# Three more means by split products: the first attention's output, the query latent, the second attention's output

## The reference, cut to what matters

```python
def rmsnorm(x, g):
    xf = x.astype(jnp.float32)
    y = xf * lax.rsqrt(jnp.mean(xf * xf, axis=-1, keepdims=True) + EPS)
    return (y * g.astype(jnp.float32)).astype(x.dtype)
...
y = jnp.concatenate([rmsnorm(ya, g[:A_WIDTH]), rmsnorm(yb, g[A_WIDTH:])], axis=-1) @ e_w_out[i]
...
q = (rmsnorm(cq, q_a_gain) @ w_uq)       # cq: the query latent, 384 wide
kv = (rmsnorm(ckv, kv_a_gain) @ w_ukv)
k_rope = rmsnorm(kr, k_gain[NOPE_DIM:])
...
y = jnp.concatenate([rmsnorm(yc, g[:C_WIDTH]), rmsnorm(yd, g[C_WIDTH:])], axis=-1) @ o_w_out[i]
```

## Time and profile before

| | us |
|---|---|
| median of 3 runs | 1103.95 (1103.93 to 1104.01) |
| the profiled execution | 1103.62 |
| its span, first to last instruction | 1101.8 |
| PE busy | 1091.3 (99%), 5148 matmul instructions |
| DVE busy | 557.4 (51%) |
| ACT busy | 426.1 (39%) |
| granted clock of PE | 1.000 |

### The profile page before, as it was taken

One profiled execution on the slowest core, in us unless ns is written; L12 is line 12 of the kernel. 1 busy time (PEld: TensorE's weight loads), 2 busy tenths in 40 slices (PEclk: granted clock), 3 DMA queues, 4 the chain that ended last, 5 costly groups with the idle time before them and its releaser, 6 DMA issues.

```text
span 1101.8 us, 13776 instructions
## 1 busy us (share of the span) xinstructions
PE 1091.3 (99%) x5148; PEld 882.0 (80%) x5148; DVE 557.4 (51%) x790; ACT 426.1 (39%) x679; POOL 104.0 (9%) x126
## 2 busy tenths in 40 slices
PE   9999999999999999999999999999999999999998
PEld 7787788888888888888878765788888888888887
DVE  6787967444344333242476589656334433453321
ACT  5756445333223222131456558545223322322110
POOL 6000000010001000000102023000001100100000
DMA  7513233333332323232233200233333233327431
GB/s 230 168 58 91 64 115 96 96 95 95 95 95 95 98 98 99 101 100 83 72 93 101 83 17 2 77 119 92 102 98 101 80 114 95 95 77 175 112 126 46
DMA packets 103241, 106.00 MB, mean 96 GB/s; under 512 B 26267, under 2 KB 79968, under 8 KB 103200
## 3 DMA queue, kind: packets, MB, share of 16 engines
q1 hardware_dynamic: 85488, 103.04, 30.2%
q10 hardware_dynamic: 16656, 2.10, 1.1%
q0 software_dynamic: 1056, 0.30, 0.1%
HBM read 101.23 MB, written 2.10 MB: 94 GB/s over the span
## 4 chain that ended last, share of the span: by engine, by line
PE 47%; DVE 2%; ACT 1%; issue 0%; ACTq 0%
PE ps L1766 15%; PE ps L1767 14%; PE ps L1768 14%; PE ps L2260 1%; PE ps L2232 1%; ACT o_p L1118 0%; PE ps L2246 0%; DVE tiny L1667 0%; DVE o_k L1595 0%; PE ps L2173 0%; PE ps L1818 0%; PE ps L1799 0%; PE ps L1811 0%; DVE o_p L1695 0%; PE ps L2103 0%
## 5 line engine op out<-in xcount | busy, mean ns | idle before, releaser
L1186 DVE TENSOR_TENSOR w_lo<-raw,w_hi 128x1024 fp32r<-128x1024 f32 (+2 forms) x192 | 224.6, 1175 | 397.6 <-ACT w_hi L727 396.0
L727 ACT ACTIVATE w_hi<-raw 128x1024 fp32r<-128x1024 f32 (+2 forms) x192 | 194.3, 1016 | 446.7 <-PE ps L1768 417.0
L1766 PE MATMUL ps<-h_hi,w_hi 128*128 128x512 f32 x912 | 357.6, 392 | 0.0
L1767 PE MATMUL ps<-h_lo,w_hi 128*128 128x512 f32 x912 | 355.1, 389 | 0.0
L1768 PE MATMUL ps<-h_hi,w_lo 128*128 128x512 f32 x912 | 355.1, 389 | 0.0
L1766 PEld LDWEIGHTS ps<-h_hi,w_hi 128*128 128x128 f32 x912 | 171.2, 188 | 39.5 <-issue 4.4
L1768 PEld LDWEIGHTS ps<-h_hi,w_lo 128*128 128x128 f32 x912 | 171.2, 188 | 36.0
L1767 PEld LDWEIGHTS ps<-h_lo,w_hi 128*128 128x128 f32 x912 | 171.2, 188 | 35.5 <-issue 0.5
L610 POOL TENSOR_TENSOR ffn_t<-ffn_t,row_scale 128x512 f32<-128x512 f32 x40 | 50.9, 1294 | 604.7 <-ACT ffn_t L941 604.7
L1767 PE MATMUL ps<-w_lo,act_hi 128*128 128x512 f32 (+1 forms) x178 | 68.8, 387 | 0.0
L1768 PE MATMUL ps<-w_hi,act_lo 128*128 128x512 f32 (+1 forms) x178 | 68.8, 387 | 0.0
(11 more groups left out here) (334 smaller groups left out, 1169.8 us busy)
## 6 DMA issues: line engine op xcount, KB each, us to landing
raw<-in_w_ffn_in SPq DMA_DIRECT2D x88, 512.0 KB, 3.5
raw<-in_w_ffn_out SPq DMA_DIRECT2D x44, 512.0 KB, 3.7
raw<-in_e_w_in SPq DMA_DIRECT2D x17, 512.0 KB, 3.8
raw<-in_o_w_in SPq DMA_DIRECT2D x8, 512.0 KB, 3.6
raw<-in_o_w_out SPq DMA_DIRECT2D x8, 512.0 KB, 3.5
raw<-in_e_w_out SPq DMA_DIRECT2D x8, 256.0 KB, 3.8
raw<-in_e_w_out SPq DMA_DIRECT2D x4, 512.0 KB, 4.1
out_tok<-x_blocks ACTq DMA_DIRECT2D x16, 128.0 KB, 2.5
```

The lines of the kernel that those rows point to most:

```text
L727: ins = act.activation(dst, src, ACT.Copy)
L1186: ins = TT(dst, src, high, ALU.subtract)
L1766: MM(dst, st_hi, mv_hi, start=start, stop=False)
L1767: MM(dst, st_hi, mv_lo, start=False, stop=False)
```

## The change

The sums of M_EB, M_CQ and M_OD get tiles for their high and low parts (`eb_sq`, `cq_sq`, `od_sq`). On ACT and DVE each gets a `sum_hi` and a `sum_lo`, ahead of the conversion of weights that stood there. On PE the three plain means become split means. That of M_EB moves from before `ab(3)` to the middle of `ab(3)`; that of M_CQ moves from after load 97 to after load 98; that of M_OD stays.

```diff
+    eb_sq = at("eb_sq", [P, 2, S], F32R, R + 20 * K)
+    cq_sq = at("cq_sq", [P, 2, S], F32R, R + 13 * K)
+    od_sq = at("od_sq", [P, 2, S], F32R, R + 16 * K)
...
-    SPLIT_SUMS = (M_MIX0, M_EQ, M_EQ + 1, M_EQ + 2, M_EQ + 3, M_EK, M_EA, M_FFN0, M_MIX1, M_CKV, M_KR, M_FFN1)
+    SPLIT_SUMS = (M_MIX0, M_EQ, M_EQ + 1, M_EQ + 2, M_EQ + 3, M_EK, M_EB, M_EA, M_FFN0, M_MIX1, M_CQ, M_CKV, M_KR, M_OD, M_FFN1)
...
@@ ACT
         through(15)
         e_out(3)
+        act.wait_ge(yb_summed, 4)
+        sum_hi(M_EB, acc[:, :])
         through(16)
         rms(M_EB, ps[:, 5, :], 512)
...
             act.activation(sq[:, j % 2, :], cq[:, j, :], ACT.Square).then_inc(cq_squared, 1)
+        act.wait_ge(cq_summed, 3)
+        sum_hi(M_CQ, acc[:, :])
         through(O_CQ + 4)
         rms(M_CQ, ps[:, 3, :], 384)
...
         through(113)
         o_out(3)
+        act.wait_ge(yd_summed, 4)
+        sum_hi(M_OD, acc[:, :])
         through(O_OUT)
         rms(M_OD, ps[:, 7, :], 512)
...
@@ DVE
         e_sum(2)
         e_sum(3)
+        dve.wait_ge(yb_summed, 4)
+        sum_lo(M_EB, acc[:, :])
         through(15)
         through(16)
         r = rms(M_EB, ps[:, 5, :], 512)
...
         sum_squares(cq_squared, cq_summed, 3, M_MIX1)
+        dve.wait_ge(cq_summed, 3)
+        sum_lo(M_CQ, acc[:, :])
         through(O_CQ + 4)
         r = rms(M_CQ, ps[:, 3, :], 384)
...
         yd_sum(3)
+        dve.wait_ge(yd_summed, 4)
+        sum_lo(M_OD, acc[:, :])
         through(O_OUT)
         r = rms(M_OD, ps[:, 7, :], 512)
...
@@ PE
         ab(2, lambda: e_values(3))
-        pe.wait_ge(yb_summed, 4)
-        mean(M_EB, 5, ones, acc[:, :])
-        ab(3)
+        ab(3, lambda: split_mean(M_EB, 5, ones_r))
...
         def cq_mean():
-            pe.wait_ge(cq_summed, 3)
-            mean(M_CQ, 3, ones, acc[:, :])
+            split_mean(M_CQ, 3, ones_r)
...
                  extra=kr_parts if j == 3 else None)
-            if j == 1:
+            if j == 2:
                 cq_mean()
...
             if (j, part) == (1, 1):
-                pe.wait_ge(yd_summed, 4)
-                mean(M_OD, 7, ones, acc[:, :])
+                split_mean(M_OD, 7, ones_r)
```

More of the change, by code:

```diff
@@ L404, in sum_parts @@
             return act_hi[:, FT - 1, :], act_lo[:, FT - 1, :]
-        t = {M_MIX0: mix0_sq, M_EK: ek_sq, M_EA: ea_sq, M_MIX1: mix1_sq, M_CKV: ckv_sq, M_KR: kr_sq}[m]
+        t = {M_MIX0: mix0_sq, M_EK: ek_sq, M_EA: ea_sq, M_MIX1: mix1_sq, M_CKV: ckv_sq, M_KR: kr_sq,
+             M_EB: eb_sq, M_CQ: cq_sq, M_OD: od_sq}[m]
         return t[:, 0, :], t[:, 1, :]
```

## The result

The changed kernel takes 1107.66 us in the median of 7 runs (1105.97 to 1109.73), the kernel before 1103.93 (1103.38 to 1104.01). The ratio is 1.0031, 95% interval 1.0022 to 1.0040. So it is slower, by 3.7 us; the forecast was 2.9. The median hides something that the single runs show, with the granted clock of PE beside them: three runs at 1.000 took 1105.97, 1106.11 and 1106.62, three at 0.998 took 1107.66, 1107.83 and 1108.09, one at 0.997 took 1109.73. The change costs about 2.2 us by itself, and in 4 of 7 runs a slower stretch of PE's clock comes on top.

A forecast was written before the change was run, and what follows sets the result against it. PE, busy 99% of the span, was taken as the bound, with other engines' chains close behind. +2.2 (M_EB) + 1.1 (M_CQ) - 0.4 (M_OD) = +2.9 us on 1103.95 gave 1106.8; range 1105.0 to 1107.9.

The forecast's parts named there:

- the clock: Rival: PE's 2.5 us stand before the first output load drops its clock, +2 us, 1108.8; chance 0.03.
- a further wait: Rival: later conversions or transfer order add 0.5 to 1.5 us on top, about 1107.9; chance 0.08.
- Prices: At the three means: split holds PE 0.46 us, plain 0.86; root starts 0.66 after a split mean, 1.16 after a plain.
- M_EB, a loss of 2.2: Mean moved into ab(3): root 2.24 us later, chain to yb_lo without slack, PE waits before the first output load.
- M_CQ, a loss of 1.1: Mean moved after load 98: PE leads by 1.56 us, chain 1.18 later; two meetings turn the lead into a loss.
- first meeting: Join product L2119 waits about 1.0 us for kr; PE's lead shrinks from 1.56 to 0.5.
- At the second: Second four of eight transposes wait for M_KR's step, 1.18 us later through load 104; lead 0.5 becomes lag 1.1.
- Part 2: The forecast's M_CQ section: loss of 1.1 us, with ends of -0.5 and +1.3.
- M_OD, a gain of 0.4: Mean split but not moved: root 0.40 us earlier, gain between 0.35 and 0.45.
- Added work at nothing: Six short ACT and DVE instructions end weight conversions 0.7 to 1.4 us later, costing nothing; at most 1.4 if wrong.
- rival with slack everywhere: Chains at yb_lo and the transposes have slack, PE keeps all savings: gain 2.4 us, 1101.6; chance 0.05.
- half case: Only M_EB's chain bites, load 104's chain absorbs 1.2: +1.3, 1105.2, chance 0.16; mirror, only M_CQ's: +0.3, 0.03.

The follow-up runs named there:

- e1: Kernel before with only M_EB's edit (split mean, moved to the middle of ab(3)): 1107.37 us, ratio 1.0032.
- e3: Kernel before with only M_OD's mean split, at its old place: 1103.53 us, ratio 0.9997.
- e6: Kernel before with only M_EB's mean split, left before ab(3): 1104.43 us, ratio 1.0006.
- e7: Kernel before with only M_CQ's mean split, left after load 97: 1105.04 us, ratio 1.0012.
- e9: Kernel before with only the conversion of load 104 moved behind the first steps of the norms: 1103.94 us, ratio 1.0001.
- e5: Kernel before with M_CQ's edit (split, after load 98) and load 104's conversion moved behind the norms' first steps: 1103.21 us, ratio 0.9995.
- e2: Kernel before with only M_CQ's edit (split mean, moved to after load 98): 1104.50 us, ratio 1.0005.
- e4: Changed kernel plus ten unused matmuls between ab(3) and the first output load: 1106.23 us, ratio 1.0024.
- e11: Changed kernel plus five unused matmuls ahead of the first output load: 1106.04 us, ratio 1.0019.
- e8: Kernel before with M_OD split, M_CQ plain in the middle of load 98, and load 104's conversion moved: 1102.29 us, ratio 0.9986.
- e10: Kernel before with M_OD split and M_CQ plain in the middle of load 98, load 104's conversion not moved: 1103.37 us, ratio 0.9996.

## Why the prediction was right, point by point

The direction, the places and the order of size came out. That the measured 1107.66 also lies within the range of 1105.0 to 1107.9, near its upper end, is in part luck: two errors went opposite ways. At full clock the change costs 2.2 us where 2.9 were forecast (near 1106.1, just under the forecast's own 1106.3 to 1107.3), and then the clock, a rival at 0.03, lifted the median by 1.6. The upper part of the range had been left for a further wait, and none came.

- *Prices.* Forecast were 0.46 us of PE for a split mean and a root 0.66 after its start. The changed kernel has 0.49, 0.47 and 0.48, and the root follows after 0.68, 0.67 and 0.68. Shown.
- *M_EB, a loss of 2.2.* The chain's shift is 2.24, the stall 2.46 and PE's own delay 2.40 - 0.14 = 2.26 in the profiled run. e1 has +1.8 in its only run at full clock; 2.24 less the 0.28 of the second attention would be 2.0, which is within the spread of single runs. The slack of at most 0.15 in that chain was the reading that decided, and it held.
- *M_CQ, a loss of 1.1.* Mis-sized: 0.66 in the trace. The distance to the kernel before is 4.01 us at the sum and 4.67 at the first `cq_hi` matmul. The first meeting is right (a lead of 0.49, 0.5 forecast, and a stall of 0.95). At the second, the chain is 0.74 late, not 1.18. The link that gave the rest back is POOL's: from its first copy to ACT's conversion passed 577.31 - 576.05 = 1.26 us before and 582.08 - 581.25 = 0.83 after. The first two rows are of the kernel before, the third is of the changed one:

```profile
575.40 1.23 DVE L1186 TENSOR_TENSOR w_lo<-raw,w_hi 128x1024 fp32r<-128x1024 f32 x1 [0.26 <-ACT w_hi L727]
...
576.05 0.66 POOL L634 COPY raw<-raw 128x48 f32<-128x48 f32 x1 [25.46 <-DMA raw<-in_o_w_uq]
```

```profile
579.13 1.23 DVE L1196 TENSOR_TENSOR w_lo<-raw,w_hi 128x1024 fp32r<-128x1024 f32 x1 [0.19 <-ACT w_hi L731]
```

  Before, POOL's copy starts while DVE subtracts to get `w_lo` of load 103, and ends at 576.71, 0.08 after DVE; in the changed kernel DVE has been done for 0.9 us, and the same copy takes 0.22. The traces of all the kernels agree. In the six that leave M_CQ at its place (before, e1, e3, e6, e7, e9) the copy meets this subtraction, takes from 0.37 to 0.80, and ends 0.08 after it each time; in the seven that move it, it does not and takes 0.22 or 0.23. So the claim of Part 2 that each link had waited only for the one before was wrong here: POOL had waited for DVE. The prediction carried a shift unchanged through six links on four engines, and named the chain over SP and POOL as what could absorb it, but not how. e5 and e9 together show that the second loss comes over load 104: with it moved the stall is gone, and the move alone gives nothing.
- *M_OD, a gain of 0.4.* 0.38 in the trace (the distance to the kernel before goes from 4.40 at the mean to 4.02 at the weight load), 0.3 in e3.
- *Added work at nothing.* No wait of PE in the trace names a converted weight.
- *The second attention, not in the sum: a gain of 0.28.* The kernel before has one more wait of PE for ACT's `o_p`. ACT stands for 0.21 us ahead of that instruction, for nothing that the profile shows:

```profile
675.18 0.69 ACT L1118 ACTIVATE o_p<-ps,tiny 128x512 f32<-128x512 f32 x1 [0.21 <-issue]
...
676.10 2.22 PE L2232 MATMUL ps<-o_k,o_q 128*64 128x448 f32 x16 [0.28 <-ACT o_p L1118]
```

  In the changed kernel both are gone, and the distance to the kernel before falls there from 4.68 to 4.40. The same holds for e1, e2, e4 to e7 and e11; e3, e8, e9 and e10 have both as before. What tells the two groups apart is whether ACT and DVE have each been given an instruction more ahead of this place, not how late PE comes. Why that helps is open.
- *The clock.* Here the forecast was wrong. It was a rival at 0.03, and it came in 4 of 7 runs, at 1.5 to 2.0 us (three runs) and about 3.5 us (one). Its price of +2 was nearly right: ten matmuls were assumed and eight were slow in the profiled run. The chance was taken from a stall of 1 us that had left the clock alone, which says nothing on one of 2.5. Without it the median would have been near 1106.1, 0.7 under the forecast of 1106.8: 0.44 by M_CQ and 0.28 by the second attention.
- *The rival with slack everywhere* and the *half case* fall by the waits for `yb_lo` and `rs`.

## What to carry to other kernels

Where the matrix engine is busy for 99%, a cheaper instruction is worth its saving only if nothing on the other engines starts from its end; so price a move by following its result to the next tile that the matrix engine reads, and compare the two arrival times before counting the saving. The one edit of the three that left its instruction in place, with its input long ready, was the one that paid. And a stall has two prices, its length and what the clock does afterwards: five useless matmuls in a stall of 2.5 us took 1.6 us off the median. Last, a delay does not pass through a chain unchanged where one of its links was being held by an engine outside the chain.

## What the runs showed of the hardware

Over all runs, the three kernels with a stall of 2.4 to 2.5 us in mid-stream (the changed one, e1, e7) had a clock below 1.000 in 14 of 24 runs. The kernel before and the nine others, whose stalls in mid-stream are at most 1.4 us (the wait at 54 us, in all of them), had it in 6 of the 185 runs whose clock is recorded. Three runs at the lower clock were profiled. In two, the changed kernel's and e1's, the slow stretch follows the stall of 2.5 us; in the third, e2's, it follows the wait at 54 us, so a shorter stall can do it too, only seldom. The loss in such a run is 1.1 to 2.5 us, and in two runs at clock 0.997 about 3.5; why it is twice as long in these is open, as none of them was profiled, and what decides whether a given run falls is not shown either. So a kernel with such a stall also has a wider spread: 3.8 us in the changed one, 0.6 in the 7 runs of the kernel before beside it.

A short copy on POOL (128x48, 0.22 us by itself) that started during DVE's subtraction of two tiles (`w_lo<-raw,w_hi`, 1.23 us) ended only 0.08 us after it, in six traces of six.
